# Six-stage layer kernel: expert buffers asked for ahead of the expert layer, the last quad of experts written out, norms by tile, and matmuls that keep TensorE busy at three seams

## What is computed

```python
for layer in range(2):
    mix = conv_mixers(x, ...) if layer == 0 else stick_breaking_attention(x, ...)
    x = layer_norm(DEEPNORM_ALPHA * x + mix, ln_mix_g[layer], ln_mix_b[layer])
    ffn = hierarchical_moe(x, ..., expert_w_up[layer], expert_w_down[layer])
    x = layer_norm(DEEPNORM_ALPHA * x + ffn, ln_ffn_g[layer], ln_ffn_b[layer])
...
x = x + ssd_dilated(rms_norm(x, norm_w)) @ w_out     # then
x = x + moba(rms_norm(x, norm_w)) @ w_out
```

## Time and profile before

| | us |
|---|---|
| median of 3 runs | 1764.6 |
| the three runs | 1765.23, 1764.6, 1761.07 |
| the profiled execution | 1764.08 |
| its span, first to last instruction | 1762.3 |
| TensorE matmul busy | 1610.9 (91%) |
| VectorE busy | 370.2 (21%) |
| ScalarE busy | 267.6 (15%) |

### The profile page before, as it was taken

How to read it: one execution, slowest core, us unless ns; L and a number is a source line. 1 busy time by engine, 2 the same in 40 slices (tenths; PEclk the granted TensorE clock), 3 DMA queues, 4 the chain that set the end, 5 groups by cost and what they waited for, 6 DMA issues and landing times.

```text
span 1762.3 us, 24213 instructions
## 1 busy us (share of the span) xinstructions
PE 1610.9 (91%) x10382; PEld 996.4 (57%) x10382; DVE 370.2 (21%) x786; ACT 267.6 (15%) x643; POOL 87.2 (5%) x152
## 2 busy tenths in 40 slices
PE   8998999889988899989998899886999999989998
PEld 7855555555555576455555555554884444645553
DVE  0932000000000212430000000003324442330322
ACT  2011000000000012210000000001232322311330
POOL 0000000000000000000000000000001233003110
PEclk9999999999999899999999999997999999999998
DMA  9529999999999932299999999998332232233100
GB/s 399 215 72 427 426 427 428 427 428 428 428 428 428 380 143 96 101 425 425 427 428 428 429 428 427 428 428 367 119 145 113 80 117 96 96 143 143 49 0 24
DMA packets 38202, 504.42 MB, mean 286 GB/s; under 512 B 4224, under 2 KB 4352, under 8 KB 6016
## 3 DMA queue, kind: packets, MB, share of 16 engines
q1 hardware_dynamic: 36992, 499.40, 68.2%
q0 software_dynamic: 1152, 4.19, 0.6%
HBM read 502.53 MB, written 1.05 MB: 286 GB/s over the span
## 4 chain that ended last, share of the span: by engine, by line
PE 75%; DMA 18%; DVE 4%; ACT 2%; issue 1%; SPq 0%; ACTq 0%; DVEq 0%
DMA ring<-in_expert_up 17%; PE ps L1061 12%; PE ps L595 11%; PE ps L712 9%; PE ps L729 7%; PE ps L774 7%; PE ps L626 5%; PE ps L695 4%; PE ps L786 3%; PE ps L1056 2%; PE ps L911 2%; PE ps L887 2%; PE ps L572 1%; PE ps L1115 1%; PE ps L893 1%
## 5 line engine op out<-in xcount | busy, mean ns | idle before, releaser
L712 PE MATMUL ps<-x_tok,constants_sb 128*128 128x256 f32 x1232 | 307.2, 392 | 0.0
L729 PE MATMUL ps<-ring,arena 128*32 128x256 f32 x3968 | 238.6, 382 | 54.7 <-DMA ring<-in_expert_up 50.4
L712 PEld LDWEIGHTS ps<-x_tok,constants_sb 128*128 128x128 f32 x1232 | 221.7, 190 | 104.9 <-issue 81.3
L1061 PE MATMUL ps<-ring,spare 128*128 128x512 f32 x480 | 213.8, 599 | 0.8 <-DVE spare L1716 0.8
L729 PEld LDWEIGHTS ps<-ring,arena 128*32 128x32 f32 x3968 | 121.2, 110 | 162.1 <-DMA ring<-in_expert_up 41.6
L595 PE MATMUL ps<-spare,ring 128*128 128x256 f32 x832 | 187.1, 389 | 2.1 <-DMA ring<-in_stream 1.3
L595 PEld LDWEIGHTS ps<-spare,ring 128*128 128x128 f32 x832 | 162.4, 196 | 25.9 <-DVE spare L1713 2.9
L1061 PEld LDWEIGHTS ps<-ring,spare 128*128 128x128 f32 x480 | 88.8, 190 | 109.3 <-issue 107.5
L774 PE MATMUL ps<-ring,arena 128*32 128x512 f32 x960 | 115.9, 598 | 13.3 <-ACT arena L1394 13.3
L1907 DVE TENSOR_TENSOR arena<-arena,ps 128x128 f32<-128x128 f32 x64 | 18.4, 288 | 516.4 <-ACT arena L1399 516.4
L626 PE MATMUL ps<-ring,arena 128*128 128x512 f32 x224 | 101.4, 610 | 1.9 <-DVE arena L2301 1.4
(11 more groups left out here) (275 smaller groups left out, 1262.5 us busy)
## 6 DMA issues: line engine op xcount, KB each, us to landing
ring<-in_expert_up SPq DMA_DIRECT2D x124, 2048.0 KB, 24.5
ring<-in_expert_down SPq DMA_DIRECT2D x46, 2048.0 KB, 26.7
ring<-in_stream SPq DMA_DIRECT2D x44, 2048.0 KB, 8.0
ring<-in_expert_down SPq DMA_DIRECT2D x28, 1024.0 KB, 24.8
arena<-in_expert_up SPq DMA_DIRECT2D x4, 2048.0 KB, 14.6
arena<-in_expert_down SPq DMA_DIRECT2D x2, 2048.0 KB, 21.8
spare<-in_expert_down SPq DMA_DIRECT2D x2, 2048.0 KB, 18.6
constants_sb<-in_constants SPq DMA_DIRECT2D x1, 1574.0 KB, 17.5
```

The lines of the kernel that those rows point to most:

```text
L712: pe.matmul(ps[:, b, 0:TOK], ident, x[:, 0, 0:TOK], start=True, stop=True, skip_group_check=True)
L729: ins = pe.matmul(ps[q * SLOTS:(q + 1) * SLOTS, 4 + e % 2, 0:TOK] .rearrange("p (g n) -> p g n", g=2), xg[:, 4 * half + k, e * SLOTS:(e + ...
L1061: ins = pe.matmul(bank(b + part), xT[:, k, part * P:(part + 1) * P], w[:, k, :], start=(k == 0), stop=(k == KT - 1))
```

## The change

The diff, cut to its core:

```diff
-                if j == EXTRA[0] and stage != first:
-                    sp.wait_ge(chunk_done, b0)
-                if j == SPARE:
+                if j == 6 and stage == MOE0 and CONV in on:
+                    sp.wait_ge(sem("cv_ya"), 1)
+                    sp.wait_ge(sem("cv_tapped"), 1)
+                    sp.wait_ge(sem("cv_convolved"), 1)
+                elif j == 8 and stage == MOE0 and CONV in on:
+                    sp.wait_ge(sem("cv_mixed"), 4)
+                elif j == 6 and stage == MOE1 and STICK in on:
+                    sp.wait_ge(sem("sk_scored"), SB_PAIRS)
+                elif j == 7 and stage == MOE1 and STICK in on:
+                    sp.wait_ge(sem("sk_o"), SB_PAIRS)
+                elif j == SPARE:
                     sp.wait_ge(sem("logits"), layer_no(stage))
...
+                def norm_rows(which):
+                    for j in range(4):
+                        r = 8 * layer + 4 * which + j
+                        ins = pe.matmul(ps[:, 4 + 2 * which + j // 2,
+                                           (j % 2) * TOK:(j % 2 + 1) * TOK],
+                                        ident[0:16, r:r + 1].broadcast_to([16, P]),
+                                        Q("ln_ffn")[0:16, :], start=True, stop=True)
+                    return ins
...
-                        if k < 3:
+                        if closing and k == 0:
+                            pe.wait_ge(s("back_moved"), i + (n2 + 1))
+                            closing()
+                        elif closing and k < 3:
+                            pe.wait_ge(sem("ln_gain_moved"), rnd + 1)
+                            spin(4, SPINS // 2)
+                        elif k < 3 and not closing:
                             spin(4)
...
-                        bias = lnr[:, 1, n * 512:(n + 1) * 512]
+                        bias = lnr[:, 1, n * 512:(n + 1) * 512] if mixer else bank(6 + n)
...
-            def rms_norm(no):
-                dve.wait_ge(sem("h_sq"), 2 * no)
-                inv_root(rstd[:, :, 0], mv[:, :, 0], 1.0 / D, RMS_EPS)
-                for t in range(2):
-                    dve.tensor_scalar(at_h[:, t], x[:, t], rstd[:, t, 0:1], None, mul)\
+            def rms_begin(no, t):
+                dve.wait_ge(sem("h_sq"), 2 * (no - 1) + t + 1)
+                rms_begun[no, t] = root_begin(rms_r[:, t], mv[:, t, 0:1], 1.0 / D, RMS_EPS, 2 + t)
+            def rms_norm(no, t):
+                root_end(rms_r[:, t], rms_begun[no, t], 2 + t)
+                for n in range(2):
+                    c = slice(n * 512, (n + 1) * 512)
+                    dve.tensor_scalar(at_h[:, t, c], x[:, t, c], rms_r[:, t, 0:1], None, mul)\
                         .then_inc(sem(f"h_ready{t}"), 1)
```

More of the change, by code:

```diff
@@ L58 @@
 ARENA = 15800
+SCRATCH = 3328
 STAGE_CHUNKS = [7, QUAD_CHUNKS * QUADS, 8, QUAD_CHUNKS * QUADS, 19, 10]
@@ L607, in tokens, with keep_warm @@
                 ins.then_inc(chunk_done, 1)
+            def keep_warm(n):
+                for _ in range(n):
+                    pe.matmul(ps[:, 5, 0:TOK], ident, con[:, 0:TOK], start=True, stop=True,
+                              skip_group_check=True)
             def residual(scale, tiles=(0, 1)):
@@ L705, in moe_round, with quad, spin @@
                 gather(1, range(0, 2) if peeled else range(4))
-                def quad(i, chunk_at):
-                    def spin(b):
-                        if not isinstance(i, int):
-                            for _ in range(SPINS):
+                def quad(i, chunk_at, opening=False, closing=None):
+                    def spin(b, n=SPINS):
+                        if not opening:
+                            for _ in range(n):
                                 pe.matmul(ps[:, b, 0:TOK], ident, x[:, 0, 0:TOK],
@@ L737, in up @@
                             ins.then_inc(chunk, 1)
-                            spin(6)
-                            if isinstance(i, int) and j == 0:
+                            if not (closing and j == 2 * QUAD - 1):
+                                spin(6)
+                            if opening and j == 0:
                                 gather(1, range(2, 4))
@@ L791, in moe_round @@
                 if peeled:
-                    quad(0, peeled)
-                with pe.Fori(1 if peeled else 0, QUADS) as i:
-                    quad(i, place)
+                    quad(0, peeled, opening=True)
+                    with pe.Fori(1, QUADS - 1) as i:
+                        quad(i, place)
+                    quad(QUADS - 1, place, closing=closing)
+                else:
+                    with pe.Fori(0, QUADS) as i:
+                        quad(i, place)
             def experts(stage, layer):
@@ L1277, in block_attention, with ready @@
                 g = base[MOBA]
[L1278 to L1280 removed]
+                def ready(t, kk):
+                    pe.wait_ge(sem(f"h_ready{t}"), (2 if SSD in on else 0) + kk + 1)
+                transposes("h5", at_h, ready, (0,))
+                if SSD in on:
+                    keep_warm(7)
+                transposes("h5", at_h, ready, (1,))
                 wait_T("h5")
@@ L1390, in moe_round, with quad @@
                 move_xg(n1 * 2 + 2)
-                with act.Fori(0, QUADS) as i:
+                def quad(i, closing=False):
                     def move_hidden(e):
@@ L1404, in moe_round @@
                     act.activation(back, ps[:, 4, 0:TOK], ACT.Copy).then_inc(s("back_moved"), 1)
-                    move_xg(i * 2 + (n1 * 2 + 4))
+                    if not closing:
+                        move_xg(i * 2 + (n1 * 2 + 4))
                     move_hidden(QUAD - 1)
+                    if closing:
+                        act.wait_ge(sem("ln_rows"), 2 * rnd + 1)
+                        act.activation(lnr[:, 0, :].rearrange("p (n c) -> p n c", n=2),
+                                       two_banks(4), ACT.Copy).then_inc(sem("ln_gain_moved"), 1)
                     act.wait_ge(chunk, i * QUAD_CHUNKS + (first_chunk + QUAD_CHUNKS))
                     act.activation(yg[:, 0:512], bank(6), ACT.Copy).then_inc(s("yg_moved"), 1)
+                with act.Fori(0, QUADS - 1 if main else QUADS) as i:
+                    quad(i)
+                if main:
+                    quad(QUADS - 1, closing=True)
             def experts(stage, layer):
@@ L1909, in moe_round @@
                             .then_inc(s("hidden"), 1)
-                    move_xg(i * 2 + (n1 * 2 + 3))
+                    if not closing:
+                        move_xg(i * 2 + (n1 * 2 + 3))
                     dve.wait_ge(chunk, i * QUAD_CHUNKS + (first_chunk + QUAD_CHUNKS))
                     dve.tensor_copy(yg[:, 512:], bank(7)).then_inc(s("yg_moved"), 1)
+                with dve.Fori(0, QUADS - 1 if main else QUADS) as i:
+                    quad(i)
+                if main:
+                    quad(QUADS - 1, closing=True)
             def experts(stage, layer):
@@ L1991, in experts @@
                                 .then_inc(sem(f"m{layer}_more_lowered"), 1)
-                layer_norm(stage)
+                if stage == MOE1 and SSD in on:
+                    layer_norm(stage, lambda: rms_begin(1, 0))
+                else:
+                    layer_norm(stage)
             def stick_breaking():
@@ L2280, in block_attention @@
                 two = SSD in on
-                rms_norm(2 if two else 1)
+                if not two:
+                    for t in range(2):
+                        rms_begin(1, t)
+                        rms_norm(1, t)
                 move_T("h5", xT, range(4), Q("norm5"))
```

203 lines of the change are left out of this document (127 added, 76 removed).

## The result

Four runs of the changed kernel stand beside four of the kernel before: medians 1748.97 us (1743.1 to 1750.59) and 1764.65 us. The ratio is 0.9917, with a 95% interval of 0.9897 to 0.9937: faster by 15.7 us. The direction was right; the size was not. 1737 was forecast, and 1748.97 lies 1 us beyond the range. In a later set the same kernel gave 1746.53 where before gave 1761.81, ratio 0.9909 (0.9893 to 0.9926).

The account below looks back on a forecast made before the run. Transfers were taken to bound the expert layers, TensorE and what feeds it the other four stages. Terms of 8.7 + 4.9 + 4.5 + 3.6 + 4.9 + 0.7 = 27.3 us off 1764.08 gave 1737, eight in ten within 1730 to 1748.

Parts of the forecast that it names:

- Prefetch: Expert layers: chunks 6 to 8 requested during the convolution let chunk 10 land earlier; 8.7 us for both layers, bounds 0 and 10.
- so the flow stays whole: Expert layers: chunk 16, asked for at 176.8, lands by 184.8, with 2.7 us in hand, so the lead survives.
- Norm rows: Expert layers: ffn gain and bias by small matmuls instead of broadcast DMAs; 4.9 us for both layers, bounds 4 and 5.3.
- Closing quad: Each expert layer's last quad: without gather and some spins TensorE ends earlier; 4.5 us for two layers, bounds 0 and 5.
- The rival that feared for the clock here: Closing quad: clock falls to half in TensorE's gaps and stays; 7.6 us slower, 1771.7 us; chance 0.03.
- Seam to stick breaking: Seam into the attention layer: bias rows and warmers keep the clock up for the projections; 3.6 us, bounds 0 and 4.2.
- so done near 591.6: Behind layer 0's scatter: the bias's four matmuls are done then, before VectorE first reads them at 593.07.
- Seam to SSD: Seam into the SSD layer: dt rows and projection chunks run at full clock; 4.9 us, bounds 1.5 and 7.
- gives nothing here: Seam into the SSD layer: norm by tile gains nothing; the four copies end at 1223.6, before at 1223.5.
- MOBA: Seam into the last layer: VectorE's four copies, no longer paced by transposes, end earlier; 0.7 us, bounds 0 and 1.5.
- The first rival: SSD seam: clock falls in spite of the warmers, 1739.5 us; with another fall moved, 3 us either way; chance 0.20.
- several terms at their low ends together: Whole kernel: several of the forecast's gains come out at their low bounds, giving 1750 to 1757 us; chance 0.06.

Follow-up runs that it names:

- e1: The kernel before with only the new arena layout and the earlier requests for chunks 6 to 8: 1753.21 us against 1760.91, ratio 0.9958.
- e11: The kernel before with TensorE's last quad written out behind its loop, same work: 1764.98 us against 1759.05, ratio 1.0027.
- e8: e3 without warmers between bias rows and branch in the stick-breaking seam, and 3 warmers behind MOBA's second transposes: 1742.55 us, ratio 0.9887.
- e4: The changed kernel without TensorE's wait for the count, its register load and the branch around further rounds: 1742.2 us, ratio 0.9898.
- e7: The changed kernel with its four calls of keep_warm removed: 1749.52 us beside 1761.07, ratio 0.9947.
- e5: e4 with the wait for the count and the register load put back, still without the branch: 1745.33 us, a single run.
- e10: The changed kernel again, unedited, in a later set: 1746.53 us, ratio 0.9909.
- e3: The changed kernel with bias rows and the 5 and 13 warmers moved ahead of the branch around further rounds: 1742.2 us, ratio 0.9887.
- e9: e8 with one warmer more before the expert layers and the SSD seam's 13 spread around branch and transposes: 1740.52 us, ratio 0.9879.

## Why the prediction was right or wrong, step by step

**What bounds the kernel: right.** A shift of the landings moved the end of the layer by as much, in e1 exactly (23.66 us from the last up landing to the scatter in both).

**Prefetch: mechanism right, size 1.5 us too large.** The forecast had chunk 10 issued near 150 and landing near 158. Timeline of SyncE and, for the two issues of that row, the DMA summaries from 149 to 151 and from 153 to 155.2 (median us to landing last):

```profile
149.99 4.04 SPq L427 DMA_DIRECT2D ring<-in_expert_down  x2
```

```profile
ring<-in_expert_down SPq DMA_DIRECT2D x1, 2048.0 KB, 7.7
```

```profile
ring<-in_expert_down SPq DMA_DIRECT2D x1, 2048.0 KB, 10.3
```

149.99 + 7.7 = 157.7; before, the same summary has 12.4, so 162.5. 4.8 us earlier, where 4.7 was worked out. (By the Trainium skill's fit, named in the prediction, the landing would have been near 157.0; the row of 8.0 us was the nearer guide.) What failed is the sentence "so the flow stays whole". It looked at chunk 16, and the hole is at chunk 11: asked for 3.7 us behind chunk 10, it lands at 153.70 + 10.3 = 164.0, not 4.9 behind 157.7. Windows of 5 us of both kernels, before first (busy times, clock, DMA share, GB/s):

```profile
150.00:155.00 5.00, 4.31 (x72) 2.92 (x72) 1.14 (x3) 0.87 (x2) 0.00 (x0) 1.00 1.05 441
```

```profile
150.00:155.00 5.00, 4.31 (x72) 2.84 (x76) 1.14 (x3) 0.88 (x2) 0.00 (x0) 1.00 0.80 279
```

The engines now have nothing but one chunk in hand for part of that stretch. Chunk 11 keeps 3.4 us of the 4.8, and all later chunks with it; the count forward in the prediction, 3.6, comes nearer to that than its 4.7, but by luck: both are for chunk 10, which gained 4.8.

**Norm rows: right.** Per layer, 6.1 us at the last quad but one less 3.5 of prefetch is 2.6; forecast 2.45. The transfers went, and that is the whole of this term. But the rows' price was put at nothing, and the bias rows, queued behind the branch, brought the wait that the prediction listed as a sign of error.

**Closing quad: wrong, 4.8 us of the miss.** Two steps failed. First, "the tail half of L774's work behind it is 1.0": a down chunk's 16 matmuls in column groups of 32 take 1.94 us when all four groups are there, but the last chunk's are split by halves, two groups each, and each half's 8 take 1.94 by themselves (the chain's row 577.23 above, and x16 in 3.94). So the quad ends 579.14 - 577.19 = 1.95 behind the tail's landing, and 1.25 was won (585.05 - 581.85 = 3.2 before, by the landing in the trace), not 2.3. Second, the landings themselves came late: TensorE's starts in the changed kernel's closing quad are

```profile
561.02 3.30 PE L802 MATMUL ps<-ring,arena 128*32 128x512 f32 x16 [1.81 <-DMA ring<-in_expert_down]
564.25 2.28 PE L899 MATMUL ps<-params_sb,constants_sb 16*128 16x256 f32 x8
567.35 2.80 PE L802 MATMUL ps<-ring,arena 128*32 128x512 f32 x16 [0.82 <-DMA ring<-in_expert_down]
572.27 1.94 PE L802 MATMUL ps<-ring,arena 128*32 128x512 f32 x16 [0.27 <-DMA ring<-in_expert_down]
```

Chunk 9 arrives 6.3 us behind chunk 8, the next one 4.9 behind that. In the stretch of 564 to 568 stands one of the new instruction transfers; in e11 the chunks landed 1.4 to 1.6 us later with such a one among them. In layer 1 it is the last up chunk that is late: TensorE waits 2.26 us for it at 1172.44, where before waits 0.95. The prediction counted the instructions that a written-out quad leaves out, and none that have to be brought in. The rival that feared for the clock here saw the right thing (3.30 and 2.80 us instead of 1.94; the granted clock is 0.50 in 562 to 564 and in 569 to 571) at the wrong price: the clock was back when the tail landed, and nothing between was late for anything.

**Seam to stick breaking: wrong, 5.2 us.** The step that failed is "so done near 591.6": the bias rows were placed straight behind the scatter, with the branch between them overlooked. Before, the branch stood in the same place, and the DMA summary from 586 to 594 has one instruction transfer too, but that stretch lay under VectorE's norm of 593.07, for which TensorE waited anyway; e8 shows that so placed it costs nothing. The change put work behind the branch that VectorE needs early, and so laid the stall open. That the warmers "delay nothing" fell with it: at half clock they end at 594. With the branch behind the rows (e8) the term measures 3.5.

**Seam to SSD: right in size, in part by luck.** 4.6 for 4.9. Chain of waits of the changed kernel:

```profile
1198.51 3.10 issue
1201.61 2.30 PE ps L899 x8
...
1214.99 27.89 PE ps L614 x128
1242.88 3.48 PE ps L1219 x32
1246.36 27.72 PE ps L614 x128
```

The dt rows take 3.48 instead of 7.01 and the four chunks 55.6; the earlier trace rows has 64.0 for the same. The stall is here too, on the chain: VectorE's first use of the bias comes at 1204.01, S + 9.20, where before has S + 7.25, so 1.95 us late. TensorE's first work on the transposed x starts at S + 20.18, where before has S + 19.89 and e4, without the branch, S + 18.23. So the norm by tile, of which the prediction says that it "gives nothing here", gives 1.7 us, and the stall, which it left out, takes 1.95: two errors that cancel. (e7, without a warmer, agrees: its bias comes 1.55 us late, at S + 8.80, and its projections at S + 19.78.) Whether the warmers hold the clock is open: e7 had it without them, e4, e5 and e8 lost 1.5 to 2 us of the first 128 matmuls with them, and e4 another 1.7 of the second 128.

**MOBA and the lottery of the clock.** The seam gave 1.7 us, more than its bound of 1.5, and they were lost when the granted clock fell to 0.50 in 1565 to 1568 (not so in e10, with 41.47 for 43.16); the fall in front of the second expert layer cost another 1.6 (L720 x24 4.57 for 2.94). The first rival had a moving fall at 3 us either way and a chance of 0.2; it should have been the normal case. Its time (1739.5) was still too good, because the two failed terms, 10.0 us together, are common to it and the forecast. Nearest came "several terms at their low ends together" (1750 to 1757), with 0.06; but both failed terms ended below their low ends of 0.

## What to carry to other kernels

Before you write a loop's last pass out or put work behind a branch, ask where its instructions come from: in a stretch in which the DMA engines are full, each such place cost 3 to 3.6 us of a standing engine, or some 1.5 us on every chunk behind it. Put a branch where its engine waits for another one anyway, and what others wait for ahead of it. And when transfers are asked for early, follow the next two requests, not only the first: the gain that stays is the smallest until the queue is full again, here chunk 11's 3.4 us and not chunk 10's 4.8.

## What the runs showed of the hardware

- Instructions are fetched while the kernel runs, in pieces of some 16 KB on a queue of its own: 43 transfers before, 49 after. A branch over a large body stalled TensorE for 2.95 to 3.64 us in five executions (the changed kernel twice, e3, e7, e9); without the branch (e4, e5) there is no stall, with the register load or without. With another wait over it (e8, seam to stick breaking) the projections start as early as without a branch.
- Two chunks of a quad with such fetches took 27.1 and 27.6 us (e11), where those of the same place took 25.6 and 26.0 before, at the same rate of bytes.
- Two groups of 32 columns take as long as four: 8 matmuls of 128x512 took 1.94 us with two groups, and 16 took 1.94 with all four.
- A 2 MB transfer on a queue that had run dry took 7.7 us, and one asked for 3.7 us behind it 10.3.
- The clock went to half after 1.8 us of idleness in the closing quad, and within 2 us behind a wait of 1.70 us ahead of MOBA's projections; in e4, e5 and e10 it stayed up there behind waits of the same length (1.69, 1.70 and 1.69). In e8 it came back in time after 2.44 us of idleness, so the length of one gap alone doesn't tell.
